# Two sequences' solve steps in one block over all quadrants, w by quadrants, scan steps in three words, and new orders, in a two-layer hybrid encoder

## The chip, the cores and the metric

The kernel runs on one core of one Trainium2 chip. The metric is the device time in microseconds of one execution. The kernel before was timed three times; a profiled execution was taken apart from these.

## The reference

The input is x of 256 tokens by 1024 channels, batch 1, in fp32. Two layers each normalise x, project it to 11808 columns, run four token mixers on them (A to D), project each mixer's 512 columns to 1024, merge the four with per-channel sigmoid gates, and add one output projection to x. Mixer A is what the change is mostly about, a bidirectional gated delta rule with 4 heads of 128 and chunks of 64 tokens:

```python
kk = einsum('bhnid,bhnjd->bhnij', k, k)
a_mat = eye(C) + where(strict, beta[..., :, None] * kk * decay, 0.0)
rhs = concatenate([v * beta[..., None], k * (beta * exp(gc))[..., None]], -1)
sol = triangular_solve(a_mat, rhs, lower=True, unit_diagonal=True)
u, w = sol[..., :dv], sol[..., dv:]
def step(state, inp):                       # once per chunk, forward and backward
    v_new = u_n - w_n @ state
    o = qd_n @ state + qk_n @ v_new
    state = state * gt_n + kd_n.T @ v_new
```

Mixer D is a bidirectional mLSTM, also in chunks of 64, with a scan of the same form; B and C are attentions.

## The kernel before

Weights stream through a ring of six 128x512 tiles. ScalarE rounds each to fp32r (`w_high`, line 1278), VectorE computes what was rounded off (`w_low`, line 1548 by a helper; both steps are the word `split`), and TensorE makes three fp32r products for each pair of tiles (lines 762 to 764). SyncE issues the loads. Everything else is laid beside that stream.

The order of work is written out by hand: the table `ORDER` has for each engine a row of words, and each word calls one function with its numbers. A word such as `b:0:2+2` is two of the eight depth steps of projection b, block 0, for both token tiles (12 products). An engine's words run strictly in this order. A word waits on semaphores for what it needs: `room` for a PSUM bank that has been emptied, `filled` for a bank that has been written, `released` for one that has been copied out.

The delta rule's four steps s (a forward chunk on one half of the partitions and a backward chunk on the other) are solved by doubling: starting from X = I - L on blocks of 2, five levels n = 1 to 5 each do X <- X - X (L_n X), and the same for X transposed. L, X and their products are 64x64 per head and direction, so a product uses one quadrant of the array, `rows_of(r)` (partitions 0 to 63 or 64 to 127) giving the row and the column half. Two heads of a step keep X on the same half, the diagonal quadrants; for the other two (`swapped`) it is on the other half, so their products use the crossed quadrants. X's transpose is never swapped. For one step and level the words are

- PE `t1` (line 946): 8 products L_n X. ScalarE copies them to SBUF (`sT1`, line 1283 by a helper), GpSimd masks L for the next level (`sLm`, line 2070).
- PE `update` (lines 957 and 962): 8 products for X (dx) and 8 for its transpose (dxt), the first left out on the last level. VectorE subtracts them from both in one operation (line 1548).

Steps 0 and 1 are solved side by side, then 2 and 3, each in a PSUM tile of two banks (`pair0`, `pair1`). After a solve `uw` computes u (line 979, 64x64 tile) and w (line 983, 64x128 tile), and ScalarE copies them. The scan has two words: `scan_v` (line 1000) and `scan_o`, which makes q times state (line 1013), qk times v_new (line 1017) and, with `kd`, the state's update (line 1027), whose second half lands in the bank that line 1017 has filled. Before a solve, `rows` (line 908) spreads a column of decay sums over 64 rows by a product of a 0/1 matrix with a diagonal that GpSimd makes (`diagonal`, line 2052); `d_rows` (line 1126) does the same for mixer D with all ones (GpSimd line 2132).

Of the kernel before, what the change touches and what calls it, by code (L numbers as in the profile page):

```python
# [13 lines left out]
P = 128  # L14
# [8 lines left out]
H = 4  # L23
# [29 lines left out]
def swapped(h, s):  # L53

    return (h >= H // 2) != (KIND_OF[s] == 1)
# [7 lines left out]
def constants():  # L63
# [9 lines left out]
    out = {"ident": eye, "ones": np.ones((P, P))}  # L73
# [6 lines left out]
    out["same"] = same  # L80
# [27 lines left out]
def const_layout():  # L108
    at, where = 0, {}
    for name, a in constants().items():  # L110
# [9 lines left out]
        turn_h.0.0 turn_h.0.1 taps za:0:0+4@0 turn_h.1.0 turn_h.1.1 za:0:4+2@0 za:0:6+2@0 za:0:0+2@1 za:0:2+4@1 za:0:6+2@1 conv:0:0+4 conv:1:0+4  # L120
        gatecols conv:2:0+4 gatecols_turn conv:3:0+4 c:0:0+2 c:0:2+2 conv:4:0+4 cols a_turn.0 a_turn.1 conv:5:0+4 c:0:4+2 c:0:6+2 c:1:0+2 a_qkt
        c:1:2+2 a_kkqk a_turn.2 c:1:4+2 rows.0 rows.1 c:1:6+2 zc:0:0+2 solve0.0 zc:0:2+2 zc:0:4+2 t1.0.1 zc:0:6+2 update.0.1 solve0.1 b:0:0+2 b:0:2+2
        rows.2 b:0:4+2 t1.1.1 t1.0.2 b:0:6+2 update.1.1 update.0.2 c_qkt t1.1.2 b:1:0+2 c_score.0.0 b:1:2+2 c_turn.0.0 c_score.0.1 t1.0.3 update.1.2
        b:1:4+2 c_mix.0.0 update.0.3 b:1:6+2 t1.1.3 t1.0.4 c_turn.0.1 c_score.1.0 update.1.3 update.0.4 b:2:0+2 t1.1.4 t1.0.5 b:2:2+2 c_mix.0.1
        b:2:4+2 c_turn.1.0 rows.3 b:2:6+2 scan_v.0 update.1.4 c_score.1.1 zb:0:0+2 update.0.5 zb:0:2+2 zb:0:4+2 c_mix.1.0 c_turn.1.1 t1.1.5 uw.0
        update.1.5 c_mix.1.1 c_out.0 zb:0:6+2 uw.1 qd.0 d:0:0+2 c_out.1 qd.1 solve0.2 solve0.3 d:0:2+2 t1.2.1 scan_o.0 t1.3.1 update.2.1 d:0:4+2
        t1.2.2 update.3.1 update.2.2 scan_v.1 t1.3.2 t1.2.3 d:0:6+2 update.3.2 update.2.3 d:1:0+2 t1.3.3 d:1:2+2 d:1:4+2 t1.2.4 update.3.3 update.2.4
        d:1:6+2 o:0:0+2 t1.3.4 scan_o.1 t1.2.5 update.3.4 update.2.5 o:0:2+2 uw.2 o:0:4+2 t1.3.5 o:0:6+2 zd:0:0+2 update.3.5 scan_v.2 qd.2 uw.3
        zd:0:2+2 scan_o.2 qd.3 zd:0:4+2 scan_v.3 zd:0:6+2 scan_o.3 gate:0,0:0+2 gate:0,0:2+2 gate:0,0:4+2 gate:0,0:6+2 gate:0,1:0+2 gate:0,1:2+2
        a_out.0 a_out.1 gate:0,1:4+2 d_rows.0 gate:0,1:6+2 d_rows.1 b_turn_in branch:0,0:0+2 branch:0,0:2+2 d_rows.2 gate:2,0:0+2 gate:2,0:2+2  # L130
        d_rows.3 gate:2,0:4+2 d_prep b_score.0.0 gate:2,0:6+2 b_score.0.1 branch:0,1:0+2 branch:0,1:2+2 b_turn.0.0 gate:2,1:0+2 gate:2,1:2+2
        b_mix.0.0 b_score.1.0 b_turn.0.1 gate:2,1:4+2 gate:2,1:6+2 b_mix.0.1 b_score.1.1 b_turn.1.0 branch:2,0:0+2 branch:2,0:2+2 b_mix.1.0
        b_turn.1.1 gate:1,0:0+2 b_mix.1.1 gate:1,0:2+2 gate:1,0:4+2 d_turn.0 d_turn.1 gate:1,0:6+2 branch:2,1:0+2 b_out.0 d_turn.2 d_turn.3
        branch:2,1:2+2 d_scan.0 gate:1,1:0+2 gate:1,1:2+2 d_scan.1 gate:1,1:4+2 b_out.1 d_scan.2 gate:1,1:6+2 branch:1,0:0+2 branch:1,0:2+2 d_scan.3
        gate:3,0:0+2 gate:3,0:2+2 gate:3,0:4+2 gate:3,0:6+2 branch:1,1:0+2 branch:1,1:2+2 gate:3,1:0+2 d_out.0 gate:3,1:2+2 d_out.1 gate:3,1:4+2
        gate:3,1:6+2 branch:3,0:0+2 branch:3,0:2+2 branch:3,1:0+2 merge_turn.0 branch:3,1:2+2 out:0:0+2 merge_turn.1 out:0:2+2 out:0:4+2 out:0:6+2
# [8 lines left out]
        turn_h.0.0 turn_h.0.1 square.1.1 split+4 turn_h.1.0 turn_h.1.1 split+1 take:za:0@0 small split+4 taps split+2 take:za:0@1 split+1  # L145
        take:conv:0@0 split+2 silu.0 split+2 take:conv:1@0 gatecols split+5 take:conv:2@0 split+4 silu.1 take:conv:3@0 gates_exp split+6 silu.2
        split+1 silu.3 split+2 cols a_turn.0 a_turn.1 a_norm.0 split+2 a_norm.1 take:conv:4@0 split+4 take:conv:5@0 take:c:0@0 take:c:0@1 split+4
        a_qkt silu.4 silu.5 a_kkqk split+1 a_turn.2 split+3 rows.0 take:c:1@0 rows.1 take:c:1@1 c_prep split+2 solve0.0 split+6 t1.0.1 take:zc:0@0
# [2035 lines left out]
```

## Time and profile before

| | us |
|---|---|
| median of three runs (lowest, highest) | 923.24 (920.37, 924.06) |
| the profiled execution's own time | 926.68 |
| its span in the trace | 924.8 |
| TensorE's matmuls busy | 889.6 |
| VectorE, ScalarE, GpSimd busy | 672.9, 499.8, 210.3 |
| granted TensorE clock over the span | 0.998 of full |

A row of groups reads: line, engine, operation, tile written <- tiles read, shape, count, then busy time and mean of one, then the engine's idle time just before such instructions and what ended it. A timeline row has start and duration in us, and in brackets the idle time before it. Matmuls overlap, so a start and the next start tell more than a duration. An fp32 product shows as two matmuls, an fp32r product or an fp32 transpose as one.

### The profile page before, as it was taken

How to read it: one execution, taken by the hardware profiler on the slowest of the kernel's cores; microseconds unless marked ns; L12 is line 12 of the kernel's file. 1: busy time of each engine (PE TensorE's matmuls, PEld its weight loads, DVE VectorE, ACT ScalarE, POOL GpSimd, SP SyncE). 2: the span in 40 equal slices, each digit the busy share in tenths (PEclk: the TensorE clock that was granted, in tenths of full speed). 3: DMA queues.
4: the chain of work that ended last, by engine and by line, in shares of the span. 5: the costliest groups of instructions: out<-in, count | busy, mean ns of one | idle time of the engine just before them, and what ended most of it. 6: DMA issues, size and time to landing. Idle time of an engine off the chain costs nothing.

```text
span 924.8 us, 18553 instructions
## 1 busy us (share of the span) xinstructions
PE 889.6 (96%) x7206; PEld 738.2 (80%) x7206; DVE 672.9 (73%) x1237; ACT 499.8 (54%) x997; POOL 210.3 (23%) x204
## 2 busy tenths in 40 slices
PE   3999999999998999999999999999999999999998
PEld 2899878888777788788879987888777877887886
DVE  4799975564557778687778999756645787696974
ACT  4467645454445366456555765554534555754552
POOL 0024321433222002313130143214414210051320
PEclk9999999999999999999999999999999999999999
DMA  9755644334369343467557655443342974244754
GB/s 253 214 177 157 196 151 126 93 105 126 105 147 209 100 128 112 138 202 212 179 161 220 181 157 175 155 116 93 105 138 81 204 184 125 87 142 137 217 171 126
DMA packets 101966, 141.05 MB, mean 153 GB/s; under 512 B 31102, under 2 KB 45558, under 8 KB 101750
## 3 DMA queue, kind: packets, MB, share of 16 engines
q1 hardware_dynamic: 101590, 139.26, 52.9%
q8 instruction: 58, 0.95, 0.4%
q10 hardware_dynamic: 288, 0.59, 0.3%
q14 instruction: 30, 0.25, 0.1%
HBM read 136.67 MB, written 7.27 MB: 156 GB/s over the span
## 4 chain that ended last, share of the span: by engine, by line
PE 85%; DVE 6%; DMA 3%; ACT 2%; SPq 2%; issue 1%; POOL 0%; DVEq 0%; ACTq 0%; POOLq 0%
PE pj L762 18%; PE pj L764 17%; PE pj L763 17%; PE mb L762 4%; PE mb L764 4%; PE mb L763 4%; PE pair L756 3%; DVE w_low L1548 3%; PE pair L962 2%; PE pair L946 2%; PE mb L756 1%; PE pair L957 1%; DVE big L1548 1%; PE mb L1102 1%; DMA mid<-in_conv_a 1%
## 5 line engine op out<-in xcount | busy, mean ns | idle before, releaser
L1278 ACT ACTIVATE w_high<-ring 128x512 fp32r<-128x512 f32 x460 | 278.6, 629 | 188.0 <-PE pj L764 115.6
L1548 DVE SCALAR_TENSOR_TENSOR w_low<-ring,w_high 128x512 fp32r<-128x512 f32 x460 | 324.4, 743 | 70.4 <-ACT w_high L1278 68.4
L762 PE MATMUL pj<-w_high,h_high 128*128 128x512 f32 x584 | 239.4, 410 | 0.2 <-DVE w_low L1548 0.2
L764 PE MATMUL pj<-w_high,h_low 128*128 128x512 f32 x584 | 228.5, 391 | 0.0
L763 PE MATMUL pj<-w_low,h_high 128*128 128x512 f32 x584 | 228.4, 391 | 0.0
L762 PEld LDWEIGHTS pj<-w_high,h_high 128*128 128x128 f32 x584 | 109.9, 188 | 27.4 <-issue 3.4
L764 PEld LDWEIGHTS pj<-w_high,h_low 128*128 128x128 f32 x584 | 109.7, 188 | 24.1
L763 PEld LDWEIGHTS pj<-w_low,h_high 128*128 128x128 f32 x584 | 110.0, 188 | 21.6 <-issue 1.0
L1283 ACT ACTIVATE big<-pair 128x512 f32<-128x512 f32 (+2 forms) x136 | 61.2, 480 | 85.7 <-PE pair L946 35.0
L2070 POOL TENSOR_TENSOR big<-big,tab 128x256 f32<-128x256 f32 x40 | 37.5, 946 | 129.9 <-PE pair L946 85.0
L2153 POOL TENSOR_TENSOR zbuf<-zbuf,mid 128x512 f32<-128x512 f32 x20 | 31.3, 1570 | 103.4 <-DVE mid L1989 103.3
L1548 DVE SCALAR_TENSOR_TENSOR big<-big,pair 128x512 f32<-128x512 f32 (+1 forms) x40 | 24.9, 630 | 35.6 <-PE pair L962 35.1
L762 PE MATMUL mb<-w_high,h_high 128*128 128x512 f32 x112 | 45.8, 409 | 0.2 <-DVE h_low L2005 0.2
L764 PE MATMUL mb<-w_high,h_low 128*128 128x512 f32 x112 | 43.8, 391 | 0.0
L763 PE MATMUL mb<-w_low,h_high 128*128 128x512 f32 x112 | 43.6, 389 | 0.0
L762 PE MATMUL pj<-w_high,y_high 128*128 128x512 f32 x88 | 35.8, 407 | 1.5 <-DVE w_low L1548 1.5
L762 PE MATMUL pj<-h_high,w_high 128*128 128x256 f32 x128 | 36.4, 284 | 0.0
L763 PE MATMUL pj<-h_low,w_high 128*128 128x256 f32 x128 | 36.2, 283 | 0.0
L764 PE MATMUL pj<-h_high,w_low 128*128 128x256 f32 x128 | 36.2, 283 | 0.0
L763 PE MATMUL pj<-w_low,y_high 128*128 128x512 f32 x88 | 34.5, 392 | 0.0
L764 PE MATMUL pj<-w_high,y_low 128*128 128x512 f32 x88 | 34.5, 392 | 0.0
L1639 DVE SCALAR_TENSOR_TENSOR big<-big,small 128x256 f32<-128x256 f32 x72 | 31.4, 502 | 0.0
(266 smaller groups left out, 1568.5 us busy)
## 6 DMA issues: line engine op xcount, KB each, us to landing
ring<-in_w_in SPq DMA_DIRECT2D x368, 256.0 KB, 3.1
ring<-in_w_branch SPq DMA_DIRECT2D x64, 256.0 KB, 3.5
ring<-in_w_out SPq DMA_DIRECT2D x32, 256.0 KB, 3.7
big<-skew SPq DMA_DIRECT2D x32, 128.0 KB, 5.9
skew<-lines SPq DMA_DIRECT2D x16, 224.0 KB
out_x<-btm SPq DMA_DIRECT2D x8, 256.0 KB, 4.1
btm<-out_x SPq DMA_DIRECT2D x8, 256.0 KB, 4.9
tab<-in_table SPq DMA_DIRECT2D x1, 1408.0 KB, 6.3
```

What stands on the lines that cost most here:

```text
L756: last = tr(bank.t[0:width, k * P:(k + 1) * P], v, ident)
L762: mm(o, r32(a), r32(b), start=start, stop=False, skip_group_check=True)
L763: mm(o, r32(a), r32(b_low), start=False, stop=False, skip_group_check=True)
L764: return mm(o, r32(a_low), r32(b), start=False, stop=stop, skip_group_check=True)
L946: last = mm(o, sLm[a, j, h], x_of(s)[a, h], start=True, stop=True)
L962: last = mm(b.t[rows_of(r), c:c + C], sT1[rows_of(r), j, h], xt_of(s)[rows_of(r), h], start=True, stop=True)
L1278: f(r32(part(u, 0)), ring[:, u % RAW], ACT.Copy).then_inc(w_rounded, 1)
L1283: f(dst, view(bank_of(key).t), ACT.Copy, scale=scale).then_inc(bank_of(key).free, 1)
L1548: return stt(o, one, 1.0, other, ALU.mult, op)
L1639: done = mark(stt(cac[:, b], cin[:, b, j:j + S], w, cac[:, b], ALU.mult, ALU.add))
L2070: pool.tensor_tensor(sLm[:, j].rearrange("p (k h) n -> p k h n", k=2), sLT[:, j].rearrange("p (k h) n -> p k h n", k=2), both, ALU.mult)\
L2153: pool.tensor_tensor(m, m, gact[i % 2][:, t], ALU.add).then_inc(merge_done, 1)
```

## The change

- **Heads.** One head of a step (`lone`) stays on the diagonal quadrants, three (`crossed`) are swapped; PSUM columns move so that diagonal and crossed products of a step stay in different banks.
- **`both(s, n)`** does the update of one step and the half-step `t1` of its partner in one word. In its order diagonal and crossed pairs alternate. `t1` alone is left at level 1 of steps 0 and 2, `update` alone at level 5 of steps 1 and 3.
- **`uw`** makes w with 64x64 tiles, and waits (semaphore `u_made`) for its own u products before it.
- **The scan** has `scan_q`, `scan_o` and `scan_k`, and mixer D's `d_q`, `d_k`, `d_o`; the state's product of A is by 64x64 tiles.
- **`rows`** is 8 products of a broadcast column with identity blocks, `d_rows` four transposes of a broadcast column; GpSimd's `diagonal` and `d_rows` and their semaphores go, and `d_rows` waits for `terms_ready`.
- **`solve0`** mixes its first two kinds of transpose; VectorE's and GpSimd's operations by head pairs become one head and three heads (GpSimd `t1`: two operations for one).
- **`ORDER`** is new on all four engines.

```diff
 def swapped(h, s):
-    return (h >= H // 2) != (KIND_OF[s] == 1)
+    return h != lone(s)
+def lone(s):
+    return H - 1 if KIND_OF[s] else 0
+def crossed(s):
+    return range(H - 1) if KIND_OF[s] else range(1, H)
...
-        b:0:4+2 t1.1.1 t1.0.2 b:0:6+2 update.1.1 update.0.2 c_qkt t1.1.2 b:1:0+2 c_score.0.0
+        b:0:4+2 b:0:6+2 both.1.1 c_qkt both.0.2 c_score.0.0 both.1.2 b:1:0+2 scan_v.0
...
+                    def both(s, n):
+                        o, m = (s + 1, n) if s % 2 == 0 else (s - 1, n + 1)
+                        update_waits(s, n)
+                        t1_waits(o, m)
+                        i, j, k = crossed(s)
+                        t1_of(o, lone(o))
+                        t1_of(o, i)
+                        dxt_of(s, 0)
+                        t1_of(o, j)
+                        dxt_of(s, 1)
+                        t1_of(o, k).then_inc(sd[o % 2].full, 1)
+                        dxt_of(s, 2)
+                        if n < LEVELS - 1:
+                            dx_of(s, i)
+                            dx_of(s, lone(s))
+                            dx_of(s, j)
+                        last = dxt_of(s, 3)
+                        if n < LEVELS - 1:
+                            last = dx_of(s, k)
+                        last.then_inc(sd[s % 2].full, 1)
...
                     def uw(s):
...
+                        last.then_inc(u_made, 1)
+                        pe.wait_ge(*at(u_made, s + 1))
                         for h in range(H):
-                            for r in range(2):
-                                n = r * 512 + 256 + h * C
-                                last = mm(b.t[:, n:n + C], vk[rows_of(r), 1, h], xt_of(s)[rows_of(r), h], start=True, stop=True)
+                            for half in range(2):
+                                for r in range(2):
+                                    n = r * 512 + 256 + h * C
+                                    last = mm(b.t[rows_of(half), n:n + C], vk[rows_of(r), 1, h, rows_of(half)], xt_of(s)[rows_of(r), h], start=True, stop=True)
...
-                        mm(sd[j].t[:, 0:H * C], K("same"), diag[s], start=True, stop=True).then_inc(sd[j].full, 1)
+                        for h in range(H):
+                            for r in range(2):
+                                column = along(cc[rows_of(r), 0, s, 0:H], C)[:, h]
+                                last = mm(sd[j].t[rows_of(r), h * C:(h + 1) * C], column, block(r), start=True, stop=True)
...
-                        mm(mb[j].t[:, :], ones, prob[:, j].rearrange("p g n -> p (g n)"), start=True, stop=True).then_inc(mb[j].full, 1)
+                        turn4(mb[j], [along(av[:, s], P)[:, h] for h in range(H)])
```

What stands in TensorE's row around the first c_score of a layer (lines 957 and 962 are the end of two updates, 756 c_qkt's transposes, 946 a half-step; each product is one row here), before:

```order
L957 MATMUL pair<-big 64x64 x2
L962 MATMUL pair<-big 64x64 x2
L756 MATMUL mb<-tab,mid 128x128 x12
L946 MATMUL pair<-big 64x64 x8
L762 MATMUL pj<-w_high,h_high 128x512
```

and in the changed kernel (766 c_qkt, 963 half-step, 977 dxt, 970 dx, 1114 c_score):

```order
L766 MATMUL mb<-tab,mid 128x128 x12
L963 MATMUL pair<-big 64x64 x4
L977 MATMUL pair<-big 64x64 x2
L963 MATMUL pair<-big 64x64 x2
L977 MATMUL pair<-big 64x64 x2
L963 MATMUL pair<-big 64x64 x2
L977 MATMUL pair<-big 64x64 x2
L970 MATMUL pair<-big 64x64 x6
L977 MATMUL pair<-big 64x64 x2
L970 MATMUL pair<-big 64x64 x2
L1114 MATMUL mb<-mid 128x256 x2
L963 MATMUL pair<-big 64x64 x4
```

The half-step stands inside the other step's update now, and the next such block follows behind the single c_score.

The second place is step 0's scan on TensorE. Before (946 half-step, 1017 qk times v_new, 1027 the state's product, 957 and 962 an update):

```order
L946 MATMUL pair<-big 64x64 x8
L1017 MATMUL mb<-big 64x128 x8
L1027 MATMUL mb<-big 128x128 x8
L946 MATMUL pair<-big 64x64 x8
L957 MATMUL pair<-big 64x64 x2
L962 MATMUL pair<-big 64x64 x2
```

In the changed kernel, where 1079 is qk times v_new, 1092 the state's product, and a projection word and a block (963, 970, 977) stand between them:

```order
L963 MATMUL pair<-big 64x64 x2
L977 MATMUL pair<-big 64x64 x2
L970 MATMUL pair<-big 64x64 x6
L977 MATMUL pair<-big 64x64 x2
L970 MATMUL pair<-big 64x64 x2
L1092 MATMUL mb<-big 64x128 x16
L963 MATMUL pair<-big 64x64 x4
L977 MATMUL pair<-big 64x64 x2
```

The state's product no longer follows line 1079 directly; a block stands on both sides of it, and it has 16 products of half the width.

## Rows read from the trace of the kernel before

**Rows 1.** The page: busy time, share of the span and instructions of each engine.

```profile
PE 889.6 (96%) x7206; PEld 738.2 (80%) x7206; DVE 672.9 (73%) x1237; ACT 499.8 (54%) x997; POOL 210.3 (23%) x204
```

**Rows 2.** Windows: stretch, length, busy time of each engine, clock, DMA share, GB/s.

```profile
45.00:120.00 75.00, 75.00 (x638) 66.74 (x638) 71.65 (x159) 50.60 (x96) 23.44 (x25) 1.00 0.60 184
120.00:200.00 80.00, 78.65 (x902) 64.63 (x901) 51.57 (x98) 40.95 (x93) 23.58 (x23) 1.00 0.39 112
200.00:290.00 90.00, 88.42 (x946) 71.62 (x944) 52.01 (x88) 40.99 (x75) 24.94 (x22) 1.00 0.56 135
```

**Rows 3.** Timeline of TensorE, two half-steps: start, duration, engine, line, operation.

```profile
155.04 0.39 PE L764 MATMUL pj<-w_high,h_low 128*128 128x512 f32 x1
155.36 0.69 PE L946 MATMUL pair<-big 64*64 64x64 f32 x32
155.98 0.50 PE L762 MATMUL pj<-w_high,h_high 128*128 128x512 f32 x1
156.32 0.39 PE L763 MATMUL pj<-w_low,h_high 128*128 128x512 f32 x1
```

**Rows 4.** The same of one update, its first row and what follows it.

```profile
145.00 0.36 PE L957 MATMUL pair<-big 64*64 64x64 f32 x8
...
145.85 0.50 PE L762 MATMUL pj<-w_high,h_high 128*128 128x512 f32 x1
```

**Rows 5.** The same of one d_rows and the second product after it.

```profile
305.71 1.02 PE L1126 MATMUL pair<-mid,tab 128*128 128x512 f32 x2
...
306.81 0.40 PE L763 MATMUL pj<-w_low,h_high 128*128 128x512 f32 x1
```

**Rows 6.** The same of four transposes.

```profile
138.69 0.60 PE L756 MATMUL mb<-tab,mid 128*128 128x128 f32 x4
139.13 1.03 PE L1049 MATMUL mb<-mid 128*128 128x256 f32 x4
```

**Rows 7.** The same of u (L979) and w (L983).

```profile
178.76 1.04 PE L979 MATMUL pair<-big 64*64 64x128 f32 x16
179.74 1.11 PE L983 MATMUL pair<-big 64*128 64x64 f32 x16
180.77 0.68 PE L962 MATMUL pair<-big 64*64 64x64 f32 x16
```

**Rows 8.** The scan's waits on TensorE and the copy it waits for, two timelines.

```profile
197.25 1.04 PE L1017 MATMUL mb<-big 64*64 64x128 f32 x16
199.09 1.16 PE L1027 MATMUL mb<-big 64*128 64x128 f32 x16 [0.79 <-ACT big L1283]
...
198.34 0.60 ACT L1283 ACTIVATE big<-mb 128x512 f32<-128x512 f32 x1 [0.78 <-PE mb L1017]
```

**Rows 9.** Who waited for whom: us in total, times, longest us.

```profile
DVE big L1548 <- PE pair L962: 35.1, 14, 5.3
...
PE mb L1027 <- ACT big L1283: 4.7, 6, 0.8
```

**Rows 10.** Timeline of TensorE, gatecols and b_turn_in of both layers.

```profile
43.92 0.36 PE L762 MATMUL mb<-h_high,y_high 128*128 128x256 f32 x1 [1.52 <-issue]
...
297.97 0.88 PE L756 MATMUL pair<-tab,btm 128*128 128x128 f32 x3 [2.77 <-ACT big L1283]
...
749.58 1.09 PE L756 MATMUL pair<-tab,btm 128*128 128x128 f32 x8 [1.14 <-DVE btm L1548]
```

**Rows 11.** Windows, layer 0's stretch with the bias loads.

```profile
280.00:290.00 10.00, 10.00 (x49) 8.26 (x48) 7.28 (x12) 4.81 (x10) 1.53 (x1) 1.00 1.14 210
290.00:300.00 10.00, 7.23 (x33) 5.62 (x32) 8.58 (x11) 6.05 (x11) 2.78 (x2) 0.87 0.92 207
```

**Rows 12.** Groups by shape: busy us, mean ns of one, idle before.

```profile
L1548 DVE SCALAR_TENSOR_TENSOR w_low<-ring,w_high 128x512 fp32r<-128x512 f32 x460 | 324.4, 743 | 70.4 <-ACT w_high L1278 68.4 <-DVE big L1589 0.7
...
L2070 POOL TENSOR_TENSOR big<-big,tab 128x256 f32<-128x256 f32 x40 | 37.5, 946 | 129.9 <-PE pair L946 85.0 <-ACT big L1427 45.0
...
L1548 DVE SCALAR_TENSOR_TENSOR big<-big,pair 128x512 f32<-128x512 f32 x32 | 21.7, 683 | 30.9 <-PE pair L962 30.4
```

More of the change, by code:

```diff
@@ L119 @@
     """, """
[L120 to L127, printed above, removed]
@@ new lines @@
+        rows.2 b:0:4+2 b:0:6+2 both.1.1 c_qkt both.0.2 c_score.0.0 both.1.2 b:1:0+2 scan_v.0 c_turn.0.0 b:1:2+2 both.0.3 c_score.0.1 both.1.3
+        b:1:4+2 b:1:6+2 c_mix.0.0 both.0.4 rows.3 c_turn.0.1 b:2:0+2 c_score.1.0 b:2:2+2 b:2:4+2 b:2:6+2 both.1.4 c_mix.0.1 both.0.5 c_turn.1.0
+        c_score.1.1 update.1.5 uw.0 zb:0:0+2 zb:0:2+2 zb:0:4+2 c_mix.1.0 qd.0 c_turn.1.1 zb:0:6+2 uw.1 solve0.2 c_mix.1.1 c_out.0 qd.1 d:0:0+2
+        c_out.1 d:0:2+2 solve0.3 t1.2.1 scan_o.0 d:0:4+2 both.2.1 scan_k.0 both.3.1 d:0:6+2 both.2.2 scan_v.1 scan_q.1 both.3.2 d:1:0+2 both.2.3
@@ L144 @@
     """, """
[L145 to L148, printed above, removed]
@@ L174 @@
-        c_score.0.0 c_score.0.1 split+7 update.1.2 update.0.3 c_mix.0.0 c_score.1.0 split+1 update.1.3 split+1 update.0.4 split+2 c_mix.0.1 split+3
-        rows_arg.3 update.1.4 split+1 cols c_sum.0 c_score.1.1 rows.2 update.0.5 rows.3 split+4 c_mix.1.0 c_mix.1.1 c_sum.1 split+1 update.1.5
-        split+1 scan_v.0 take:zb:0@0 take:zb:0@1 solve0.2 split+1 solve0.3 split+2 gain_a split+2 update.2.1 split+2 scan_o.0 update.3.1 update.2.2
-        split+1 update.3.2 split+1 update.2.3 split+5 update.3.3 update.2.4 scan_v.1 split+8 update.3.4 update.2.5 split+3 scan_o.1 split+2
@@ L186 @@
[L186 removed]
+        turn_h.0.0 turn_h.0.1 split+2 scale.1 split+2 turn_h.1.0 take:za:0@0 turn_h.1.1 split+2 taps split+1 small split+1 take:za:0@1 split+4 conv.0
+        split+4 conv.1 split+6 conv.2 split+2 silu.0 conv.3 split+3 gates_in split+1 gates_out silu.1 silu.2 silu.3 split+4 a_norm.0 split+3 a_norm.1
+        split+5 conv.4 a_scale split+2 conv.5 silu.4 silu.5 cols split+4 rows_arg.0 split+1 rows_arg.1 rows.0 split+1 rows.1 split+6 c_prep split+2
@@ new lines @@
+        take:zc:0@0 take:zc:0@1 split+1 update.0.1 c_rotate.0 split+2 rows_arg.2 split+1 c_rotate.1 update.1.1 update.0.2 split+2 c_score.0.0
+        update.1.2 split+4 update.0.3 c_score.0.1 split+4 update.1.3 update.0.4 c_mix.0.0 rows.2 split+1 rows_arg.3 split+3 c_score.1.0 split+2
+        rows.3 split+3 update.1.4 c_mix.0.1 update.0.5 split+2 update.1.5 c_score.1.1 split+2 gain_a split+2 solve0.2 c_mix.1.0 c_sum.0 split+2
+        take:zb:0@0 take:zb:0@1 scan_v.0 c_mix.1.1 c_sum.1 split+2 solve0.3 split+3 update.2.1 scan_o.0 update.3.1 split+3 update.2.2 update.3.2
@@ new lines @@
+        scan_v.1 split+1 update.2.3 split+2 update.3.3 split+2 update.2.4 split+2 update.3.4 update.2.5 split+4 scan_o.1 b_square.0 scan_v.2 split+1
+        b_square.1 split+2 update.3.5 split+2 b_prep.0 split+1 scan_o.2 scan_v.3 split+3 a_add.0 split+2 a_add.1 split+1 take:zd:0@0 a_sum.0
+        take:zd:0@1 split+5 a_sum.1 split+3 a_gate.0 a_gate.1 split+2 d_prep split+4 y_parts.0 b_prep.1 split+2 window split+6 take:branch:0,0@0
+        d_rows.0 d_rows.1 split+2 d_rows.2 d_rows.3 split+2 d_max d_arg.0 split+2 take:branch:0,0@1 split+4 d_arg.1 d_arg.2 take:branch:0,1@0
```

318 lines of the change are left out of this document (163 added, 155 removed).

## The prediction

> **What bounds the kernel now.** I read the shares of the engines first, then the waits, then the timeline of TensorE. TensorE's matmuls are busy 889.6 of 924.8 us, VectorE 672.9, ScalarE 499.8 [rows 1]. Shares can hide a stretch with another limit, so the windows come next: between 120 and 290 us, where most of the changed code runs, TensorE is busy 78.65 of 80 and 88.42 of 90 us and VectorE about 52 in each; between 45 and 120 us VectorE is busy 71.65 of 75, but TensorE has no gap there either [rows 2]. So almost everywhere the end is set by the length of TensorE's queue, and an edit is worth what it takes out of that queue, plus the few waits of TensorE itself.
>
> **Unit prices.** An fp32 product on a 64x64 quadrant counts as two matmuls. Two half-steps in a row (32 matmuls) run from 155.36 until the projection starts at 155.98, 0.62 us; one update (32 matmuls too) runs from 145.00 to 145.85, 0.85 us [rows 3, 4]. With four quadrants working side by side, the two half-steps keep each quadrant for four products. An update is 16 products. It keeps the two diagonal quadrants for six (four heads of X^T, two of X) and the others for two. Hence 0.85 - 0.62 = 0.23 us for two products, 0.115 us for one, which I call a slot, and 0.16 us for leaving the 64x64 size. Entering costs 155.36 - 155.04 = 0.32 instead of the usual 0.23, so 0.09; a visit costs 0.25 us beside its work. The first projection after it takes 156.32 - 155.98 = 0.34 instead of 0.23, a restart of 0.11 us [rows 3].
>
> **1. Solve in one block.** Counted over both layers, before: 40 half-steps of 2 slots, 32 updates of 6 and 8 last ones of 4, 304 slots. After: with one head on the diagonal and three crossed, the diagonal quadrants take 4 (X^T) + 1 (X) + 1 (half-step) and the crossed ones 3 + 3, so a block has 6 slots; 32 such blocks, 4 of the last level of 5, 4 lone half-steps of 3, 4 last updates of 4: 240 slots. 64 x 0.115 = -7.4 us. solve0 keeps its slots (7 + 1 either way: seven for its two transposes and one moved between them); VectorE's three small operations there only change width.
>
> **2. Fewer visits.** In TensorE's order the size of the array's tile changes 206 times before and 160 times after, 23 visits less, 5.7 us; runs of fp32r products start 124 times before and 108 after, 16 x 0.11 = 1.8 us. Together -7.5 us.
>
> **3. d_rows by transposing.** The product with ones keeps TensorE from 305.71 to 306.81 with the next projection, 1.10 - 0.23 = 0.87 us with its restart [rows 5]. Four transposes take 139.13 - 138.69 = 0.44 [rows 6], with a restart of about 0.05 on top: -0.4 us, eight times, -3.2 us. GpSimd's multiplication for it and for `diagonal` goes; GpSimd is busy 210 us and I give nothing for it. rows(s) was a pass over 256 columns of 2 x 0.22; it is now 8 products, 4 slots, 0.46: nothing.
>
> **4. w by quadrants.** w's 16 matmuls run from 179.74 to 180.77 [rows 7]; of these 1.03 us some 0.13 is a change of size, counted in 2, which leaves 0.90 of work. On four quadrants they are 4 slots, 0.46 us: -0.44 x 8 = -3.5 us.
>
> **5. The wait between u and w** (u_made) is new. TensorE waits for its own last product. Queued behind it are w and all that follows. The trace has no such wait. Its lower bound is the 0.05 that lies between two pairs anyhow, so nothing; the upper bound is the longest wait of this kind, scan_o's 0.79 us idle, which holds a ScalarE copy of 0.60 [rows 8]. Less that copy, 0.2 us is left for two signals; one signal plus the drain of the last 128-column product (0.27 us long, [rows 7]) makes about 0.35: +2.8 us over eight.
>
> **6. The scan in three words.** In front of the state's product TensorE waits for ScalarE to empty the bank that scan_o has just filled: 4.7 us in six waits [rows 8, 9]. In all six places a block, an update or u and w now stand between them, 0.7 us or more with the visit: -4.7 us. The state's product by quadrants is 16 x 2 passes over four quadrants, 0.9 us as before.
>
> **7. Other orders.** gatecols waited 1.52 us in layer 0 for parameters [rows 10] and comes 11 us later: -1.5. b_turn_in waited 2.77 us in layer 0 and 1.14 in layer 1 [rows 10], behind weight splits and b_prep; b_prep.1 now stands right behind y_parts.0 and b_turn_in one projection word later. In layer 0 ScalarE waits for weights' DMAs there, with the DMA engines 92% to 114% busy [rows 11], which no order mends; of 3.9 us I take 1.5.
>
> Gains: 7.4 + 7.5 + 3.2 + 3.5 + 4.7 + 1.5 + 1.5 = 29.3; less 2.8 for the new wait, 26.5 us.
>
> **What becomes late next.** The answer to a block is the drain of its last products (0.22 us, [rows 4]), VectorE's subtraction of 0.683 us [rows 12] and two signals of about 0.1: some 1.1 us from the last start, and 0.37 more on the mean (half a split of 0.743, [rows 12]) if VectorE has just begun a split. In the new order ten pairs of blocks have only a c_score, a c_mix, scan_k or scan_o between them, 0.9 to 1.1 us with the visits: I take 0.4 us each, 4 us. The RoPE rows reach c_qkt later, since c_rotate.1 stands behind rows_arg.2 and a split: 0.6 us twice. t1.2.5's copy on ScalarE stands behind two squares and four splits: 0.5 twice. That is 6.2 us of new waits, between 0 (if the copies come first) and 18 (ten pairs at the full 1.1 + 0.7 us of a whole split ahead). GpSimd's masking is two operations for one of 0.946 us [rows 12], but stands a whole block ahead of its use.
>
> Sum: 26.5 - 6.2 = 20.3 us. The profiled run took 926.68 us of its own with a span of 924.8, 3.4 us over the median of 923.24. Taken from the median: 923.24 - 20.3 = 902.9, say 903 us.
>
> **Rivals.** *Given back in part.* The waits are moved rather than removed: VectorE, busy 95% of 45 to 120 us, and the DMA-bound piece near 290 us hold what the rest has won. Then the orders of 7 bring nothing and the new waits are 11 us rather than 6.2: 923.2 - (26.5 - 3.0) + 11 = 911 us. Against it: VectorE idles 28 of the 80 us from 120 to 200, where the slots go [rows 2].
>
> *Quadrants don't overlap across two sequences.* A block writes four banks, and the two row halves write one bank at a time. The Trainium skill, "TensorEngine Tiling (Array Packing)", Gotcha 1: PSUM Pressure, says that different row tiles cannot access the same PSUM bank at once. Here u's 16 matmuls, two row halves into one bank, take 179.74 - 178.76 = 0.98 us [rows 7], while one behind another, at the 0.11 us that 128 columns take in [rows 6], they would take 1.8: this trace disagrees, they overlap, though to different partitions. If the block's crossed and diagonal products did exclude each other, it would have 12 slots rather than 6: 36 blocks x 0.7 = +25 us on 903, 928 us; with a part of them overlapping, about 922, no change.
>
> *The two sequences chained together: slower.* Each block now waits for both sequences, where before a late one let the other go first. At 0.9 us each (the answer's 1.47 less some half a microsecond of other work between) 36 blocks lose 32 us in place of 6.2: 923.2 - 26.5 + 32 = 929 us. It decides if VectorE comes to the subtraction a split or more late nearly everywhere; the point at which it eats the whole gain is 26.5 / 36 = 0.74 us a block. For it: 36 strict waits. Against: 22 of the 36 blocks have a projection word (12 products of 0.23, 2.7 us) or more between them and the block before, and ahead of the old subtractions VectorE idled 35.1 us in 14 waits [rows 9], so it comes early.
>
> *The change doesn't do what it says*: the four lone half-steps and 36 blocks stand in TensorE's order as described, so this gets nothing.
>
> **Chances.** Forecast 0.66 (range 893 to 908), given back in part 0.22, quadrants excluding each other 0.06, chained and slower 0.06. About 0.5% (4.6 us) is what a measurement of this kernel tells from no change. Faster by over 0.5%: 0.66 + 0.22 = 0.88; within: 0.06, most of the third case; slower: 0.06. The range: below, no new waits at all (-6.2), the waits of 7 gone in full (5.4 rather than 3.0) and the wait of 5 at its lower bound (-2.8) make 891.6, rounded to 890; above, the orders of 7 bring nothing (+3.0), the new waits are 13 us (+6.8) and the wait of 5 is 0.5 us (+1.2): 914.
>
> **What would show it.** A block: 6 slots, about 0.70 us between a change of size at each end, 0.85 to the projection. 36 of them, 18 a layer. u's matmuls, then a gap of 0.35 us, then w in 0.46. d_rows with four transposes in 0.44. No wait of the state's product on ScalarE. The waits of TensorE for VectorE's subtraction, absent now, 4 to 6 us in all. TensorE busy near 868 us and still 96% of the span. Wrong if a block takes over 0.8 us without a wait in it, if the gap before w is over 0.5 us, or if TensorE's waits for answers of blocks pass 12 us.

## The result and the profile after

| | before | after |
|---|---|---|
| median of five runs (lowest, highest), us | 923.24 (920.37, 925.14) | 910.24 (906.83, 916.08) |
| the profiled execution's own time, us | 926.68 | 916.08 |
| its span, us | 924.8 | 914.3 |
| TensorE's matmuls busy, us | 889.6 | 873.7 |
| granted TensorE clock over the span | 0.998 | 0.993 |

The change makes the kernel faster: the ratio of the times is 0.986 with a 95% interval of 0.9835 to 0.9884, 13 us. The forecast was 903 us, a gain of 20.3. The profiled execution is the slowest of the five; in the other four the granted clock was 0.996 to 0.998. The engines of the page, which answer to [rows 1]:

```profile
PE 873.7 (96%) x7558; PEld 729.9 (80%) x7558; DVE 652.8 (71%) x1237; ACT 496.0 (54%) x997; POOL 180.0 (20%) x228
```

TensorE is busy 15.9 us less and idle 914.3 - 873.7 = 40.6 us instead of 35.2. Part of the busy time is a slow clock: 0.7% of 914.3 us is 6.4 us, against 0.2%, 1.8 us, before (estimates, upper ones, since part of the slow stretches was idle in both). So at full clock the queue has become about 15.9 + 4.6 = 20.5 us shorter, and 5.4 us of idle time and some 4.6 us of slow clock took half of that back in this execution.

**The changed code itself.** The timeline of TensorE in the changed kernel: two blocks with c_score between them (963 is the half-step and starts a block; the rows inside the blocks are left out), u (1033) and w (1040), four transposes of d_rows, and the state's product (1092) with the block behind it. They answer to [rows 3 to 8].

```profile
142.46 0.34 PE L963 MATMUL pair<-big 64*64 64x64 f32 x8
...
143.31 1.13 PE L1114 MATMUL mb<-mid 128*128 128x256 f32 x4
144.39 0.34 PE L963 MATMUL pair<-big 64*64 64x64 f32 x8
...
145.25 0.50 PE L772 MATMUL pj<-w_high,h_high 128*128 128x512 f32 x1
...
170.68 1.04 PE L1033 MATMUL pair<-big 64*64 64x128 f32 x16
171.79 0.69 PE L1040 MATMUL pair<-big 64*64 64x64 f32 x32
172.41 0.50 PE L772 MATMUL pj<-w_high,h_high 128*128 128x512 f32 x1
...
292.23 0.60 PE L766 MATMUL pair<-tab,small 128*128 128x128 f32 x4
292.59 0.48 PE L772 MATMUL pj<-w_high,y_high 128*128 128x512 f32 x1
...
201.66 1.07 PE L1092 MATMUL mb<-big 64*64 64x128 f32 x32
202.85 0.34 PE L963 MATMUL pair<-big 64*64 64x64 f32 x8
```

A block takes 144.39 to 145.25, 0.86 us to the projection, in all places where a projection follows it (0.73 on the last level, where dx is left out). w takes 0.62 us to the projection, with its change of size, and stands 1.11 us behind u's start. d_rows takes 0.36 us (292.23 to 292.59). The state's product has no wait; the block after it starts 1.19 us behind it, some 0.3 us later than its work of 0.9 explains.

**Where TensorE waits now.** The table of who waited for whom (us, times, longest), leaving out the start of layer 0; it answers to [rows 9]:

```profile
PE pair L766 <- ACT big L1354: 7.8, 2, 4.6
PE pj L772 <- DVE w_low L1620: 2.9, 1, 2.9
PE mb L772 <- ACT mid L1400: 2.9, 1, 2.9
PE pj L772 <- ACT mid L1400: 2.5, 2, 1.5
PE pair L921 <- ACT big L1354: 2.3, 4, 0.9
```

The same waits in the timeline, with the idle time in brackets. The two of line 766 are b_turn_in, as in [rows 10]; those on line 1400 are a projection that waits for ScalarE to empty a bank; the one at 49.81 waits for a weight split.

```profile
49.81 0.36 PE L772 MATMUL pj<-h_high,w_high 128*128 128x256 f32 x1 [2.87 <-DVE w_low L1620]
...
277.06 0.51 PE L772 MATMUL pj<-w_high,h_high 128*128 128x512 f32 x1 [1.01 <-ACT mid L1400]
...
291.33 1.07 PE L766 MATMUL pair<-tab,btm 128*128 128x128 f32 x8 [3.11 <-ACT big L1354]
...
430.10 0.79 PE L772 MATMUL mb<-w_high,y_high 128*128 128x512 f32 x1 [2.87 <-ACT mid L1400]
...
722.65 0.50 PE L772 MATMUL pj<-w_high,h_high 128*128 128x512 f32 x1 [1.53 <-ACT mid L1400]
...
738.46 1.94 PE L766 MATMUL pair<-tab,btm 128*128 128x128 f32 x8 [4.65 <-ACT big L1354]
```

Six waits hold 16.0 us. What ScalarE does ahead of the one at 291.33:

```profile
284.64 0.64 ACT L1349 ACTIVATE w_high<-ring 128x512 fp32r<-128x512 f32 x1 [1.19 <-PE pj L774]
286.54 0.63 ACT L1349 ACTIVATE w_high<-ring 128x512 fp32r<-128x512 f32 x1 [1.27 <-DMA ring<-in_w_branch]
288.31 0.63 ACT L1349 ACTIVATE w_high<-ring 128x512 fp32r<-128x512 f32 x1 [1.14 <-DMA ring<-in_w_branch]
290.07 0.63 ACT L1349 ACTIVATE w_high<-ring 128x512 fp32r<-128x512 f32 x1 [1.13 <-DMA ring<-in_w_in]
290.61 1.07 ACT L1354 ACTIVATE big<-pair 128x512 f32<-128x512 f32 x2
```

TensorE starts b_turn_in at 287.19 and needs ScalarE's copy (line 1354) to go on. In ScalarE's row this copy stands behind eight weight splits. The last three of them wait for their weights' DMAs, which come one every 1.76 us; the one before, at 284.64, waits for a product of TensorE. The copy starts at 290.61. Windows of the changed kernel, with the columns of [rows 2] (length, busy time of the engines, granted clock, DMA share, GB/s); the second and third answer to [rows 11]:

```profile
46.00:56.00 10.00, 7.13 (x47) 6.96 (x47) 10.00 (x22) 4.74 (x9) 1.20 (x2) 0.83 0.58 166
280.00:290.00 10.00, 8.22 (x41) 6.67 (x39) 7.59 (x12) 4.97 (x8) 0.00 (x0) 1.00 1.15 218
290.00:300.00 10.00, 8.67 (x47) 7.40 (x48) 5.26 (x9) 6.71 (x12) 0.00 (x0) 1.00 0.80 234
425.00:436.00 11.00, 8.13 (x29) 6.27 (x28) 4.23 (x7) 4.58 (x8) 0.55 (x1) 0.84 0.84 252
735.00:745.00 10.00, 6.54 (x24) 5.73 (x25) 2.15 (x4) 5.16 (x10) 0.00 (x0) 0.66 0.71 189
```

The DMA share is 1.15 in 280 to 290 us (a packet's whole time is counted in the window in which it starts, so the share can pass 1). And where TensorE has just stood still for 2.87 or 4.65 us, its granted clock is 0.83, 0.84 and 0.66 of full, averaged over the window: the 512-column matmuls that start 0.23 us apart elsewhere, at 2.4 GHz, start 0.43 us apart after 430.69 and after 741.48, at 1.2 GHz. The wait of 3.11 us did not bring this (1.00 in 290 to 300 us).

### The profile page after: what moved, and what is told of

It reads as the page before. It is cut to its first block, busy times and chain, and to the rows that moved or that the text cites. A ratio compares the mean times of both kernels' runs of the same rounds, so it can differ in the third digit from the quotient of the medians.

```text
span 914.3 us, 19289 instructions
## 1 busy us (share of the span) xinstructions
PE 873.7 (96%) x7558; PEld 729.9 (80%) x7558; DVE 652.8 (71%) x1237; ACT 496.0 (54%) x997; POOL 180.0 (20%) x228
## 4 chain that ended last, share of the span: by engine, by line
PE 86%; DMA 6%; DVE 3%; ACT 2%; SPq 2%; issue 1%; ACTq 0%
PE pj L772 18%; PE pj L774 17%; PE pj L773 17%; PE pair L766 4%; PE mb L772 4%; PE mb L774 4%; PE mb L773 4%; DMA ring<-in_w_in 4%; DVE w_low L1620 2%; PE pair L977 2%; PE pair L963 2%; PE mb L1167 2%; DMA ring<-in_w_branch 1%; PE mb L766 1%; ACT big L1354 1%
## 5 line engine op out<-in xcount | busy, mean ns | idle before, releaser
L1620 DVE SCALAR_TENSOR_TENSOR w_low<-ring,w_high 128x512 fp32r<-128x512 f32 x460 | 320.3, 732 | 97.8 <-ACT w_high L1349 97.2
L772 PE MATMUL pj<-w_high,h_high 128*128 128x512 f32 x584 | 236.3, 405 | 2.6 <-ACT mid L1400 2.5
L2133 POOL TENSOR_TENSOR big<-big,tab 128x64 f32<-128x64 f32 x80 | 41.9, 544 | 126.7 <-PE pair L963 78.2
```

The source lines that it names most:

```text
L772: mm(o, r32(a), r32(b), start=start, stop=False, skip_group_check=True)
L1620: return stt(o, one, 1.0, other, ALU.mult, op)
L2133: last = pool.tensor_tensor(sLm[:, j, heads_of], sLT[:, j, heads_of], over(level, heads_of.stop - heads_of.start), ALU.mult)
```

## The experiments

Each ran in five rounds beside the kernel before. The ratio is to the kernel before on the same chip, with its 95% interval; two experiments are compared by these ratios, times 923 us.

| | median us | ratio | interval |
|---|---|---|---|
| the changed kernel | 910.24 | 0.9860 | 0.9835, 0.9884 |
| old_orders | 922.82 | 0.9999 | 0.9983, 1.0016 |
| turn_early | 906.59 | 0.9814 | 0.9791, 0.9836 |
| takes_early | 923.00 | 0.9997 | 0.9983, 1.0011 |
| bias_half | 898.53 | 0.9727 | 0.9705, 0.9749 |
| serial_bias | 909.25 | 0.9844 | 0.9829, 0.9860 |
| wwide_bias | 902.14 | 0.9769 | 0.9755, 0.9782 |
| scan_bias | 906.35 | 0.9818 | 0.9804, 0.9833 |
| before_bias | 921.61 | 0.9979 | 0.9969, 0.9989 |
| conv_bias | 899.05 | 0.9756 | 0.9734, 0.9778 |
| rows_bias | 898.46 | 0.9737 | 0.9719, 0.9755 |
| tail_bias | 898.42 | 0.9736 | 0.9717, 0.9756 |
| rows_tail_bias | 897.79 | 0.9714 | 0.9701, 0.9728 |

Two theories on the lost 7 us. **A:** the order of ScalarE's row holds TensorE, with splits ahead of copies that TensorE needs first. **B:** the DMA engines hold it, because the bias loads of mixer B go out with the weights in just that stretch.

### old_orders: the new functions in the orders of the kernel before

The table of all four engines is that of before, with `scan_q`, `scan_o`, `scan_k` in a row where `scan_o` stood (`d_scan` in the same way), and `update` makes both of its products:

```diff
 def update(s, n):
     update_waits(s, n)
     for h in range(H):
         last = dxt_of(s, h)
+    if n < LEVELS - 1:
+        for h in (lone(s), *crossed(s)):
+            last = dx_of(s, h)
     last.then_inc(sd[s % 2].full, 1)
...
-        ... b:0:4+2 b:0:6+2 both.1.1 c_qkt both.0.2 c_score.0.0 both.1.2 ...
+        ... b:0:4+2 t1.1.1 t1.0.2 b:0:6+2 update.1.1 update.0.2 c_qkt t1.1.2 b:1:0+2 c_score.0.0 ...
```

> The changed kernel's functions (heads one and three, w by quadrants with its wait, d_rows by transposes, state's product by quadrants) run in the orders of the kernel before: no block of two sequences, every half-step and update a visit of its own, the state's product again right behind line 1079. By the terms of my sum this keeps only 3 (-3.2), 4 (-3.5) and 5 (+2.8), so about 919 us, 0.5% below before. If the functions are worth nothing by themselves and all of the 13 us comes from blocks and orders, it is 923. If it is as fast as the changed kernel (910), the blocks and the orders have brought nothing.

Measured 922.82 us, no difference from before, so the functions alone bring nothing. The 4 us that I expected left something out: outside a block the heads one and three cost slots. Two half-steps in a row and the projection behind them in this kernel, which answers to [rows 3]:

```profile
155.67 0.93 PE L964 MATMUL pair<-big 64*64 64x64 f32 x32
156.53 0.50 PE L773 MATMUL pj<-w_high,h_high 128*128 128x512 f32 x1
```

They take 0.86 us here and 0.62 before, one slot more each, 40 x 0.115 = +4.6 us, which a block fills with the other sequence's work. An update has one slot fewer on the diagonal quadrants by the same count, and yet a single one takes 0.91 us to the projection here (145.05 to 145.96) and 0.85 before. TensorE is busy 888.7 us, as long as before (889.6). In front of the state's product TensorE waits some 0.8 us again in six places, 4.7 us, as in [rows 8]. So the gain of the changed kernel comes from the blocks and the orders, with the functions as what makes the blocks possible.

### turn_early: ScalarE's b_turn_in four splits earlier

```diff
-        ... y_parts.0 split+8 b_turn_in take:gate:0,1@0 take:gate:0,1@1 split+10 d_prep ...
+        ... y_parts.0 split+4 b_turn_in take:gate:0,1@0 take:gate:0,1@1 split+4 split+10 d_prep ...
```

> ScalarE's b_turn_in and the two copies of gate block 0,1 stand four weight splits earlier in its row; nothing else changes. Theory A (the order of ScalarE's row holds TensorE): the two waits inside b_turn_in, 3.1 us in layer 0 and 4.65 us in layer 1 of the changed kernel's trace, go, and with the one of 4.65 us the slow clock behind it (0.66 in 735 to 745); the splits come late by the length of two copies only, so the kernel gains 6 to 9 us, 902 us. Theory B (the DMA engines hold it): TensorE then waits for the branch weights instead and the time stays at 909 to 910 us.

906.59 us, 4 us below the changed kernel: more than B in its pure form allows, less than A asks for. The timeline of TensorE and, behind the second dots, of ScalarE in this kernel (765 is b_turn_in, 771 a product with branch weights, 1353 the copy, 1348 a split):

```profile
287.44 1.07 PE L765 MATMUL pair<-tab,btm 128*128 128x128 f32 x8 [0.34 <-ACT big L1353]
...
291.46 0.50 PE L771 MATMUL pj<-w_high,y_high 128*128 128x512 f32 x1 [1.82 <-DVE w_low L1619]
...
286.70 1.09 ACT L1353 ACTIVATE big<-pair 128x512 f32<-128x512 f32 x2 [4.68 <-PE pair L765]
...
290.03 2.73 ACT L1348 ACTIVATE w_high<-ring 128x512 fp32r<-128x512 f32 x5
```

The wait of 3.11 us has become 0.34, as A says; and 4 us later TensorE stands 1.82 us for a split of the branch's weights. That looks like B, but ScalarE's rows say otherwise: it stood 4.68 us for TensorE's b_turn_in with five splits queued behind the copies, and these then ran in a row, without a wait for a DMA. Their weights had landed. The new wait comes from the row again, which now has the copies too early. The same numbers come back in layer 1. So this run shows that the row matters, and leaves open what the transfers cost.

### takes_early: two more groups of copies four splits earlier

```diff
-        ... split+10 take:gate:0,0@0 take:gate:0,0@1 a_out.0 ...
+        ... split+6 take:gate:0,0@0 take:gate:0,0@1 split+4 a_out.0 ...
-        ... y_parts.3 split+5 take:gate:3,1@0 take:gate:3,1@1 split+4 ...
+        ... y_parts.3 split+1 take:gate:3,1@0 take:gate:3,1@1 split+4 split+4 ...
```

> As turn_early, and ScalarE's copies of gate block 0,0 and of gate block 3,1 also stand four splits earlier. Theory A: the waits of a projection for those copies go as well (1.0 us near 277, 1.5 near 722, 2.9 near 430 with the slow clock of 0.83 behind it), another 4 to 6 us below turn_early. Theory B: the weights that are awaited instead come as late, nothing below turn_early.

923.0 us, 17 us above turn_early: a plain miss of both theories. Timelines of TensorE and, behind the dots, ScalarE in this kernel:

```profile
276.50 0.66 PE L764 MATMUL pair<-tab,big 128*128 128x128 f32 x4 [3.26 <-DVE big L1844]
...
431.06 0.80 PE L770 MATMUL pj<-w_high,y_high 128*128 128x512 f32 x1 [3.07 <-DVE y_low L1618]
...
271.92 0.60 ACT L1398 ACTIVATE mid<-pj 128x512 f32<-128x512 f32 x1 [4.29 <-PE pj L772]
...
273.77 2.18 ACT L1347 ACTIVATE w_high<-ring 128x512 fp32r<-128x512 f32 x4
```

Now ScalarE waits 4.29 us for TensorE's products, with four splits queued behind (273.77), VectorE's halves of these splits and the gating of mixer A (line 1844) come behind them in its own row, and a_out waits for that, 3.26 us in each layer; at the tail it is 3.07 us for y_low, in each layer. These waits make 12.7 of the 17 us; the granted clock is lower too, 0.991 over the span against 0.995 in turn_early, some 4 us. The same row of ScalarE can be too late and too early; for these two groups the slack between the two is under four splits.

### bias_half: the bias loads behind every second weight unit

```diff
-                        if 0 <= after < 2 * NT * STEPS:
-                            load_bias(after)
+                        if after % 2 == 0 and 0 <= after // 2 < 2 * NT * STEPS:
+                            load_bias(after // 2)
```

> The changed kernel with mixer B's 16 bias loads of a layer issued behind every second weight unit instead of every one. Weights arrive every 1.76 us near 285 and TensorE uses one in 1.38 us. Theory B (the DMA engines hold this stretch): the weights arrive in time, ScalarE reaches b_turn_in early by itself, and the waits of 1.0, 3.1, 1.5 and 4.65 us shrink to under 2 in all: 902 us. Theory A in its pure form (ScalarE's row alone, whatever the DMA) gives 908 to 910 us. Both can be true at once: the row makes TensorE wait for splits that it does not need yet, and the DMA makes those splits late; then this run and turn_early each remove most of the same waits.

898.53 us, 12 us below the changed kernel and more than B asked for. ScalarE's row is the one of the changed kernel, word for word, and yet its copy comes in time. The timeline of TensorE at b_turn_in and, behind the dots, of ScalarE in this kernel:

```profile
286.83 1.07 PE L766 MATMUL pair<-tab,btm 128*128 128x128 f32 x8 [0.34 <-ACT big L1354]
...
279.05 3.22 ACT L1349 ACTIVATE w_high<-ring 128x512 fp32r<-128x512 f32 x6
...
286.09 1.08 ACT L1354 ACTIVATE big<-pair 128x512 f32<-128x512 f32 x2 [0.43 <-PE pair L766]
```

Its window of 280 to 290 us, with the columns as above:

```profile
280.00:290.00 10.00, 9.66 (x53) 8.12 (x52) 7.80 (x13) 7.12 (x14) 0.00 (x0) 1.00 0.78 202
```

And the engines on its page:

```profile
PE 868.2 (97%) x7558; PEld 726.1 (81%) x7558; DVE 651.9 (73%) x1237; ACT 495.1 (55%) x997; POOL 178.7 (20%) x228
```

The DMA share is 0.78 rather than 1.15, six splits run in a row, and the waits of 1.0, 3.1, 1.5 and 4.65 us of the changed kernel are 0.3 or gone. They sum to 10.3 us, and the wait at 430.10 shrinks from 2.87 to 1.6. The two profiled executions, 916.08 and 899.98 us, are 16.1 us apart: 10.9 us of these waits and, at 0.993 against 0.997 of the clock, some 3.7 us of slow clock make up 14.6. So in this row of ScalarE the late transfers are the cause, and its order is how their lateness reaches TensorE before TensorE needs the weights themselves. Whether another order alone, b_turn_in two splits earlier rather than four, would have brought as much was not run.

### before_bias: the same edit on the kernel before

> The kernel before with the bias loads behind every second weight unit and nothing else. Theory B says that the DMA engines become the bound only once TensorE's queue is short enough and ScalarE's row has splits ahead of b_turn_in: before waited 2.77 and 1.14 us there, so it gains at most 3.9 us and I expect 2.5, 920.5 us. If the loads cost the kernel before as much as the changed one (11.7 us), it is 911.5 us, and the change has nothing to do with what they cost.

921.61 us, 2 us below before (0.9979, 0.9969 to 0.9989). The loads cost the kernel before 2 us and the changed one 12. With them out of the way on both sides the change is worth 0.9979 - 0.9727 = 2.5%, 23 us.

### serial_bias: the order of products inside a block

```diff
-                        i, j, k = crossed(s)
                         t1_of(o, lone(o))
-                        t1_of(o, i)
-                        dxt_of(s, 0)
-                        t1_of(o, j)
...
+                        for h in crossed(o):
+                            last = t1_of(o, h)
+                        last.then_inc(sd[o % 2].full, 1)
+                        for h in range(H):
+                            last = dxt_of(s, h)
+                        if n < LEVELS - 1:
+                            for h in (lone(s), *crossed(s)):
+                                last = dx_of(s, h)
```

> bias_half, with the products of a block in the old order: all of the half-step, then all for X transposed, then all for X, instead of diagonal and crossed pairs in turn. The words and the visits stay the same, so this prices only how the quadrants overlap inside a block. If TensorE starts products strictly in order, a block keeps 9 slots instead of 6 (the crossed quadrants wait while four pairs go to the diagonal ones, and the other way round): 36 x 3 x 0.115 = +12 us, 910 us. If each quadrant had a queue of its own the order would not matter: 898.5 us.

909.25 us, 1.2% or 10.8 us above bias_half. A block of this kernel, and the projection behind it (rows inside left out):

```profile
136.33 0.40 PE L963 MATMUL pair<-big 64*64 64x64 f32 x10
...
137.43 0.50 PE L772 MATMUL pj<-w_high,h_high 128*128 128x512 f32 x1
```

1.10 us rather than 0.86: the order of the products counts, as it would if TensorE starts them strictly in order, and 32 x 0.24 and, for the last level's blocks (0.80 rather than 0.73), 4 x 0.07, 8.0 us of the 10.8, are seen directly. It is two slots a full block, not the three that I had counted. So nearly half of the 23 us that the change is worth with the loads out of the way hangs on the order of products inside one word.

### wwide_bias: w by 64x128 tiles again

```diff
-                        last.then_inc(u_made, 1)
-                        pe.wait_ge(*at(u_made, s + 1))
                         for h in range(H):
-                            for half in range(2):
-                                for r in range(2):
-                                    ...
-                                    last = mm(b.t[rows_of(half), n:n + C], vk[rows_of(r), 1, h, rows_of(half)], ...
+                            for r in range(2):
+                                ...
+                                last = mm(b.t[:, n:n + C], vk[rows_of(r), 1, h], xt_of(s)[rows_of(r), h], start=True, stop=True)
```

> bias_half with w undone: w by 64x128 tiles straight behind u, without the wait for u's products. By terms 4, 2 and 5 of the sum (0.44 of work and 0.25 of a change of size each way less the wait, which the changed kernel's trace shows as 0.31 us idle): 8 x (0.44 + 0.25 - 0.3) = +3 us, 901.5 us. If the wait has eaten what the quadrants bring: 898.5 us or below.

902.14 us, 0.42% or 3.9 us above bias_half. u and w of this kernel:

```profile
170.67 1.04 PE L1033 MATMUL pair<-big 64*64 64x128 f32 x16
171.64 1.11 PE L1037 MATMUL pair<-big 64*128 64x64 f32 x16
172.68 0.50 PE L772 MATMUL pj<-w_high,h_high 128*128 128x512 f32 x1
```

u's start to the projection is 2.01 us here and 1.73 in the changed kernel: 8 x 0.28 = 2.2 us. The intervals of the two ratios are 0.14 to 0.22% wide on each side, so the other 1.7 us are not told from chance.

### scan_bias: scan_k directly behind scan_o, steps 0 and 2

```diff
-        ... scan_o.0 d:0:4+2 both.2.1 scan_k.0 ...
+        ... scan_o.0 scan_k.0 d:0:4+2 both.2.1 ...
-        ... scan_o.2 uw.3 scan_k.2 ...
+        ... scan_o.2 scan_k.2 uw.3 ...
```

> bias_half with scan_k directly behind scan_o in steps 0 and 2 of each layer (not in step 1, where ScalarE's copy stands behind a block that would then never start). By term 6 each of the four places waits 0.79 us again for ScalarE's copy: +3.2 us, 901.7 us; step 0 also changes one visit of the 64x64 size less, -0.25 us twice. If the word apart has only moved the wait elsewhere: 898.5 us.

906.35 us, 0.91% or 8.4 us above bias_half, over twice what I expected. The waits in the timeline:

```profile
199.66 1.10 PE L1092 MATMUL mb<-big 64*64 64x128 f32 x32 [1.13 <-ACT big L1354]
...
205.60 0.34 PE L963 MATMUL pair<-big 64*64 64x64 f32 x8 [1.01 <-DVE big L1620]
```

The wait for the copy is 1.13 us at step 0 (a split stands ahead of it on ScalarE) and 0.79 at step 2, 3.8 us in four places. And scan_k had been the cover between both.2.1 and both.3.1: without it the second waits 1.01 us for VectorE's subtraction, 2.0 us in two places. These make 5.9 of the 8.4 us; the rest is not explained.

### conv_bias, rows_bias, tail_bias and rows_tail_bias: the waits that are left

The first pair of lines is conv_bias, the second rows_bias, the third tail_bias; rows_tail_bias has the last two. All stand on bias_half.

```diff
-        ... split+6 conv.2 split+2 silu.0 ...
+        ... split+7 conv.2 split+1 silu.0 ...
-        ... a_turn.2 rows.0 rows.1 c:1:6+2 zc:0:0+2 ...
+        ... a_turn.2 c:1:6+1 rows.0 rows.1 c:1:7+1 zc:0:0+2 ...
-        ... y_parts.3 split+5 take:gate:3,1@0 take:gate:3,1@1 split+4 ...
+        ... y_parts.3 split+3 take:gate:3,1@0 take:gate:3,1@1 split+2 split+4 ...
```

> bias_half with VectorE's conv.2 (ten small operations, 6 us) one weight split later. In layer 0 TensorE waits 2.77 us near 47 for the split that stands behind conv.2, and its clock is 0.83 after it. If the place in VectorE's row is the cause, the wait shrinks to what VectorE, busy all of 46 to 56 us, can't make up, about 1.5 us, and the clock stays up: -2 to -3 us, 896 us. If VectorE's total work there is the cause, the wait only moves to the next split: 898.5 us.

> bias_half with rows.0 and rows.1 one weight unit later (between the two halves of a projection word). They wait 0.89 us in each layer for ScalarE to empty the bank that a_turn.2 has just filled. If solve0 behind them has half a microsecond of slack, -1.8 us less a restart of 0.1 twice: 897 us. If solve0 is late by the same time, 898.5 us.

> bias_half with ScalarE's copies of gate block 3,1 two weight splits earlier (takes_early had them four earlier, and there a wait of 3.07 us for VectorE's y_low in both layers took the place of one of 2.9 in layer 0). If two splits are inside the slack on both sides: -1.6 us, 897 us. If ScalarE then waits for TensorE as in takes_early: 900 us or above.

> bias_half with the edits of rows_bias and tail_bias together. Their traces show the waits of 0.89 us twice and of 1.6 us gone, yet each alone came out at 898.4 us, as bias_half did. If the waits are truly gone and only the measurement hid it, both together give 3 us: 895.5 us. If what they remove comes back elsewhere, 898.5 us again.

conv_bias: 899.05 us, no gain (2.7 us above bias_half by the ratios, within their intervals). The wait in TensorE's timeline has only shrunk from 2.77 us to this:

```profile
49.97 0.36 PE L772 MATMUL pj<-h_high,w_high 128*128 128x256 f32 x1 [2.25 <-DVE w_low L1620]
```

The window of 45 to 56 us in bias_half:

```profile
45.00:56.00 11.00, 8.23 (x56) 8.05 (x56) 11.00 (x24) 5.26 (x10) 1.68 (x2) 0.84 0.62 182
```

and in conv_bias, where the clock stays up in the profiled execution:

```profile
45.00:56.00 11.00, 8.75 (x73) 8.57 (x72) 10.31 (x19) 6.01 (x11) 3.15 (x4) 1.00 0.70 198
```

VectorE is busy 11.00 of 11 us there in bias_half, so its work as a whole may be the bound rather than the place of conv.2; no run took work out of it, and this is not shown. rows_bias and tail_bias: the waits that they aimed at are gone in their traces, but at 898.46 and 898.42 us, with intervals of 0.2% on each side, neither is told from bias_half. Both together give 897.79 us, 0.9714 (0.9701 to 0.9728), 1.2 us below bias_half by the ratios and again within the intervals. This is the fastest version that ran, 2.9% below before.

## Why the prediction was right or wrong, step by step

- **What bounds the kernel** (TensorE's queue): right for most of the span, wrong in one stretch of each layer, 270 to 292 and 715 to 738 us, where the weights arrive every 1.76 us or later and TensorE uses a unit in 6 x 0.23 = 1.38.
- **1 and 2, solve in blocks and fewer visits** (-7.4, -7.5): right. The block takes 0.86 us to the projection, 0.85 was forecast. serial_bias shows that this holds only with diagonal and crossed pairs in turn.
- **3, d_rows** (-3.2): 0.36 us for four transposes rather than 0.44; right.
- **4 and 5, w and its wait** (-3.5, +2.8): together -0.7 of net, and with the change of size that 2 counted about -2.7 us; the trace shows 2.2, wwide_bias 3.9 (not sharp). TensorE's weight loads sit idle 2.5 us in the eight waits, 0.31 each, and w's first product starts 0.34 us behind the last of u; 0.35 was forecast. (The 0.27 and 0.22 us that the forecast takes for one product are right, but [rows 7] and [rows 4] show merged rows and not these.)
- **6, the scan** (-4.7): right, no wait of the state's product is left in the changed kernel, and scan_bias shows that four of the six are worth 3.8 us and the word more than that, as cover between two blocks.
- Terms 1 to 4 gave 21.6 us of queue; the profile shows 20.5 at full clock, and TensorE busy 868.2 us in bias_half, where 868 was forecast for the changed kernel.
- **New waits for answers of blocks** (+6.2): less. Behind the single scan words of layers 0 and 1 (202.85 above is one) a block starts some 0.3 us late in four places, 1.2 us; the other short gaps cost nothing that the trace shows. rows.0 waits 0.89 us in each layer for ScalarE, which I had not seen: a_turn.2 stands directly ahead of it now; rows.3, behind a block, waits 0.24. c_qkt's extra 0.6 us did not come: it waits 0.6 us in each layer, as before.
- **7, the orders: the step that failed.** I wrote that ScalarE waits for weights' DMAs there, "which no order mends; of 3.9 us I take 1.5" as a gain. The waits of b_turn_in grew from 3.9 to 7.8 us, and 2.5 + 2.9 us of waits for ScalarE's copies of gate blocks came beside them. I had read [rows 11], 114% of the DMA engines, as a limit on the gain and not as a bound that a shorter queue would run into, and every split that ScalarE's new row puts ahead of a copy hands that lateness on. With the loads spaced out and the same row, b_turn_in's waits are 0.7 us (bias_half). gatecols' 1.52 us went as forecast, but the projection at 49.81 waits 2.87 us instead, where VectorE is busy all of 46 to 56 us.
- **Not in the sum at all: the clock.** Three waits of 2.87 to 4.65 us were followed by a granted clock of 0.66 to 0.84 in windows of 10 and 11 us, some 4.6 us more than before in the profiled execution. The rows had a sign of it: 0.87 in 290 to 300 us [rows 11], behind b_turn_in's wait of 2.77 us [rows 10].

The forecast of 903 us was 7 us too low. The measured 910.24 us lies inside the range that was added up, 890 to 914, and outside the 893 to 908 that the chances gave the forecast itself; the two had not been made to agree. With the loads spaced out on both sides the change is worth 23 us, more than the 20.3 forecast, so what is missing was lost to the late transfers and what followed from them, and not in the queue.

The rival "given back in part" named both places, VectorE between 45 and 120 us and the DMA-bound piece near 290, and its 911 us is what came out (910.24). That number was luck in part: its terms raised the waits for answers of blocks, which stayed small, and had neither the growth of b_turn_in's waits nor the clock. Of the other rivals, the quadrants do overlap across two sequences: a block takes 0.86 us, as 6 slots make it, and would take some 0.7 more if crossed and diagonal products excluded each other. The Trainium skill, "TensorEngine Tiling (Array Packing)", Gotcha 1: PSUM Pressure, has row tiles unable to access one PSUM bank at once; no such exclusion shows in this trace. And the blocks did not chain the two sequences: the trace has four waits of some 0.3 us ahead of a block.

## What to carry to other kernels

A shorter queue on the bounding engine is worth what the transfers behind it can deliver: compare, stretch by stretch, the time between arrivals of weights with the time in which they are used, before and after the edit. In an in-order row every copy behind prefetching work inherits that work's lateness, so a prefetch that is late costs before its data is needed; and a copy that stands too early holds up prefetching whose data has landed (turn_early, takes_early). Spread the small-packet loads first, and reorder after that. When quadrants are to overlap, alternate them in the instruction order, and price the layout in the order in which it will run: the same layout brought nothing in the old one.

## What the runs showed of the hardware

- Waits of 2.87, 2.87 and 4.65 us were followed by the lower clock level (granted clock 0.83, 0.84 and 0.66 in the windows around them), one of 3.11 us was not (1.00). In turn_early a wait of 1.82 us stands at the same place of both layers; the lower level follows it in layer 0 and not in layer 1 (windows of that kernel around the two):

```profile
290.00:300.00 10.00, 8.54 (x32) 6.87 (x33) 7.44 (x14) 5.28 (x10) 0.00 (x0) 0.83 0.62 187
730.00:740.00 10.00, 8.18 (x44) 6.63 (x43) 6.65 (x13) 7.24 (x14) 0.00 (x0) 1.00 0.70 190
```

  The length of the wait alone therefore does not tell it, and what else does stays open.
- A wait of TensorE for its own products left its weight loads idle for 0.31 us between u and w, eight times alike.
- A bias load of 128 KB in short rows (64 fp32 values each) costs the DMA engines more than its bytes say: with one beside each weight unit of 256 KB the share of 280 to 290 us is 1.15 at 218 GB/s; with one beside every second it is 0.78 at 202 GB/s, in the window shown with bias_half.
